# Expert gates kept in DRAM by fours of steps instead of pairs

## The chip, the cores and the metric

The kernel runs on 1 core of one Trainium2 chip. The metric is the device time of one execution in microseconds (us), as the median of several runs. Engines are named as in the profile: PE is TensorE (PEld its weight loads), DVE VectorE, ACT ScalarE, POOL GpSimd, SP the SyncE queue that issues most DMAs. L12 is line 12 of the kernel.

## What is computed

The reference is one step of a two-layer backbone over 640 tokens (128 of context, 512 latent) of width 1024. Each layer has a mixing part (gMLP and mLSTM heads) and a PEER part: every token chooses 8 x 16 of 16384 single-neuron experts by product keys. The change touches the PEER part only:

```python
idx = jnp.take_along_axis(cand_idx.reshape(T, PEER_HEADS, -1), pos, axis=-1)
gate = jax.nn.softmax(best, axis=-1).astype(h.dtype)

def block(args):
    tb, ib, gb = args
    act = jax.nn.gelu(jnp.einsum('td,thkd->thk', tb, expert_u[ib]))
    return jnp.einsum('thk,thkd->td', gb * act, expert_v[ib])
```

## The kernel before, in words

The PEER part of a layer is done in two ways at once. For 336 tokens (`NX`, the dense ones) all 16384 experts are computed, in 128 steps of 128 experts. For the other 304 (`X0` = 48 and two tiles) the rows of `peer_u` and `peer_v` are gathered one per token and choice.

**The gates.** A dense token needs a gate for each expert, zero for nearly all. They are made ahead of the 128 steps. DVE compares the chosen keys with `iota_k` (L1890, two one-hots per group of 8 tokens, in `hot1` and `hot2`), ACT and POOL multiply one of them by the gates (L1636, L2115), PE multiplies the two (L1519), and ACT evacuates the result (L1623) into `gate_s`. That is 42 groups, seven to a block of 56 tokens (`KEPT`), six blocks. Blocks 0 to 4 are stored to `gate_dram` (`store`, L1353 to L1357), and the last stays in SBUF. `gate_dram` is laid out by steps: an entry for two steps holds, for each of the 128 partitions, five blocks of 2 x 56 gates. A store thus writes 64 x 128 runs of 448 bytes, and a load of a pair (`gate_pair`, L1338) 128 rows of 2240 bytes.

**A step j.** PE makes the scores (`scores`, L1529), ACT the gelu (L1649) into `gelu_s`, DVE multiplies by the gates (`weigh`, L1901 for the 280 columns from DRAM, L1903 for the 56 kept ones) into `h_s`, and PE adds the products to PSUM (`products`, L1537 and L1542). PE's order is scores j+1, products j. The expert tiles come in through SP: `scores_of` (L1343) loads u when the scores two steps before are done (`s_a`), `values_of` (L1344) loads v when the products two steps before are done (`s_g2`). Both have two buffers. A gate pair is loaded by `gates_of`, each second step, when the weights of the pair before last are done (`s_h`). All of this stands in one queue, in the order of the code, so a wait holds everything behind it.

**The gathers.** POOL issues indirect DMAs of 128 rows of 4096 bytes, 512 KB each, into two rings of 8 slots: u (L2130) and v (L2141). DVE takes the dot of a u row (L1915) or adds a v row (L1933). Each such operation frees a slot and lets POOL issue the next row. `gathered_done` spreads the 608 operations of a layer over the steps: four a step up to step 18 (`STEADY`), then some five, fewer in the four steps of `HEAVY`. DVE does them in its program order, between `weigh(j)` and `weigh(j + 1)`.

**Into the steps.** PE's scores wait until ACT has evacuated the last group (`s_fe`). POOL's first eight u rows wait for the third store of the even buffer (`s_gst[0]`, the fifth store). SP waits for all stores, loads gate pairs 0 and 1, and then v of step 0.

Of the kernel before, what the change touches and what calls it, by code (L numbers as in the profile page):

```python
# [11 lines left out]
F32 = mybir.dt.float32  # L12
U32 = mybir.dt.uint32
# [4 lines left out]
P = 128  # L18
D = 1024
# [31 lines left out]
KEPT = NX // BLOCKS  # L51
GW = NX - KEPT
BY_BLOCK = KEPT // OCT
FIRST_AT, NEXT_AT = 0, 24
SLOTS = 80
HIDDEN = TOPK - P // SHARES
# [64 lines left out]
def build(nc, io):  # L121
# [3 lines left out]
    def sb(name, shape, dt=F32):  # L125
        return ctx.enter_context(nc.sbuf_tensor(name, shape, dt))
# [8 lines left out]
    with ctx:  # L135
# [1 line left out]
        x_res = sb("x_res", [P, TILES, D])  # L137
        y_nat = sb("y_nat", [P, TILES, D])
        big = sb("big", [P, 32000])
        gates_area = sb("gates_area", [P, 4480])  # L140
        kn_area = sb("kn_area", [P, 2560])
        ident = sb("ident", [P, P])
        ones_row = sb("ones_row", [ROWS, P])
# [18 lines left out]
        spare = sb("spare", [P, 2])  # L162
        iota_k = sb("iota_k", [P, N_KEYS])
        gate_rows = nc.dram_tensor("gate_rows", (2 * DEPTH, 2 * D), F32, kind="Internal").ap()
        gate_dram = nc.dram_tensor("expert_gates", (N_KEYS // 2, P, 2 * GW), F32, kind="Internal").ap()
        late_rows = nc.dram_tensor("late_rows", (2, P, D), F32, kind="Internal").ap()
        ctx_scores = nc.dram_tensor("context_scores", (P, 2 * D), F32, kind="Internal").ap()
        share_idx = nc.dram_tensor("share_experts", (XA, P), U32, kind="Internal").ap()
# [91 lines left out]
        eq_4 = wgate_flat  # L260

        u_ring = [big[:, 5120 + n * D:5120 + (n + 1) * D] for n in range(USLOTS - 1)] + [big[:, 19456:20480]]
        v_ring = carve(big, 21504, VSLOTS, D)
        acc = big[:, 29696:30720]
        s_cin = sem("condition_loaded")
        v_s = [big[:, 30720:31744], y_nat[:, 2, :]]
        u_s = [y_nat[:, n, :].rearrange("p (k e) -> p k e", e=P) for n in range(2)]
        gelu_s = [gates_area[:, 2560 + n * NX:2560 + (n + 1) * NX] for n in range(2)]
        h_s = [gates_area[:, 2560 + n * NX:2560 + (n + 1) * NX] for n in (2, 3)]
        g_s = [big[:, 20480:20480 + 2 * GW], gates_area[:, 2560 + 4 * NX:2560 + 4 * NX + 2 * GW]]  # L270
        part_idx = carve(kn_area, 2048, 1, P // PARTS, dt=U32)
        part_gate = carve(kn_area, 2048 + P // PARTS, 1, P // PARTS)
        a_idx = kn_area[:, 2048 + 2 * P // PARTS:2048 + 2 * P // PARTS + XA].bitcast(U32)
        a_gate = kn_area[:, 2048 + 2 * P // PARTS + XA:2048 + 2 * P // PARTS + 2 * XA]
        y_turned = carve(big, 5120, KD, 2 * P)
        fw = wgate_flat
        act_c = kn_area[:, 2432:2432 + TOPK]
# [30 lines left out]
        for l in range(DEPTH):  # L308
# [1024 lines left out]
            landed = lambda u, k, slots: l * rows_before(UNITS, 0) // slots + rows_before(u, k) // slots + 1  # L1333
            by_ranks = lambda v: v.rearrange("p (a b) -> p a b", b=TOPK)

            def gate_pair(sp, q, place):

                sp.dma_start(g_s[place], gate_dram[bass.ds(q, 1)].rearrange("a p t -> p (a t)")).then_inc(s_gs[place], 16)  # L1338

# [6 lines left out]
            with nc.Block() as block:  # L1346
                @block.sync
                def _(sp):
                    mix_sync(sp)
                    u0, v0 = stream(sp, 0, 0)  # L1350
                    u1, v1 = stream(sp, 1, 1)

                    def store(b):  # L1353

                        sp.wait_ge(s_fe, BY_BLOCK * (b + 1))
                        sp.dma_start(gate_dram[:, :, 2 * KEPT * b:2 * KEPT * (b + 1)].rearrange("q p t -> p q t"),
                                     gate_s[b % 2].rearrange("p (q s) t -> p q (s t)", s=2)).then_inc(s_gst[b % 2], 16)  # L1357

                    def scores_of(j, par, past):

                        sp.wait_ge(s_a, past)
                        stream(sp, j, par)[0]()

                    def values_of(j, par, past):

                        sp.wait_ge(s_g2, past)
                        stream(sp, j, par)[1]()

                    sp.wait_ge(s_nat, NG + 1)
                    sp.dma_start(part_rows[:, :], y_nat[0:X0, 0, :]).then_inc(s_qs, 16)  # L1370
                    for n in range(NG):
                        sp.dma_start(late_rows[n], y_nat[:, GATHERED[n], :]).then_inc(s_qs, 16)
                    sp.wait_ge(s_qs, 16 * (1 + NG))
                    for t in range(XA):
                        sp.dma_start(y_nat[SHARES * t:SHARES * (t + 1), CTX, :],
                                     part_rows[XB + t:XB + t + 1, :].broadcast_to([SHARES, D])).then_inc(s_qr, 16)
                    for part in range(PARTS):
                        sp.dma_start(y_nat[XB * part:XB * (part + 1), G0, :], part_rows[0:XB, :]).then_inc(s_qr, 16)
                    sp.wait_ge(s_s, 4 * PH)
                    sp.dma_start(gate_b.rearrange("p c d -> p (c d)"),  # L1380
                                 gate_rows[2 * l + 1:2 * l + 2].broadcast_to([P, 2 * D])).then_inc(s_grl, 16)
                    sp.wait_ge(s_sbe, 2 * PH)
                    sp.dma_start(ctx_scores.rearrange("p (g k) -> p g k", k=P), sc_b[:, 1, :, :]).then_inc(s_qs, 16)
                    sp.wait_ge(s_rk, 1)
                    u0()
                    u1()
                    v1()
                    sp.dma_start(share_idx[:, :], exp_idx[XB:X0, 0, :]).then_inc(s_qs, 16)
                    sp.dma_start(share_gate[:, :], exp_gate[XB:X0, 0, :]).then_inc(s_qs, 16)
                    for part in range(PARTS):  # L1390
                        at, slots = slice(XB * part, XB * (part + 1)), slice(P // PARTS * part, P // PARTS * (part + 1))
                        sp.dma_start(part_idx[at, 0, :], exp_idx[0:XB, 0, slots]).then_inc(s_qd, 16)
                        sp.dma_start(part_gate[at, 0, :], exp_gate[0:XB, 0, slots]).then_inc(s_qd, 16)
                    sp.wait_ge(s_qs, 16 * (NG + 4))
                    sp.dma_start(a_idx, share_idx.rearrange("t (s r) -> (t s) r", r=XA)).then_inc(s_qd, 16)
                    sp.dma_start(a_gate, share_gate.rearrange("t (s r) -> (t s) r", r=XA)).then_inc(s_qd, 16)
                    for b in range(BLOCKS - 1):
                        store(b)
                    sp.wait_ge(s_gst[0], 16 * 3)
                    sp.wait_ge(s_gst[1], 16 * 2)  # L1400
                    gate_pair(sp, 0, 0)
                    gate_pair(sp, 1, 1)
                    sp.wait_ge(s_sbe, 2 * PH + 1)
                    v0()
                    def gates_of(q, place):

                        sp.wait_ge(s_h, 2 * q - 2)
                        gate_pair(sp, q, place)

                    scores_of(2, 0, 1)  # L1410
                    with sp.Fori(0, N_KEYS // 4 - 1) as m:
                        for n in range(4):
                            scores_of(3 + 4 * m + n, 1 - n % 2, 2 + 4 * m + n)
                            if n % 2 == 0:
                                gates_of(2 + 2 * m + n // 2, n // 2)
                            values_of(2 + 4 * m + n, n % 2, 1 + 4 * m + n)
                    scores_of(N_KEYS - 1, 1, N_KEYS - 2)
                    values_of(N_KEYS - 2, 0, N_KEYS - 3)
                    values_of(N_KEYS - 1, 1, N_KEYS - 2)
                    if not final:  # L1420
                        next_weights(sp, l + 1)
                        sp.wait_ge(s_wg, (8 if first else 4) * 16)
                    else:
                        sp.dma_start(fw, io["final_norm_w"].broadcast_to([P, D])).then_inc(s_in, 16)
                        for n, t in enumerate(TAIL):
                            if t in GATHERED:
                                sp.wait_ge(s_xg, n + 1)
                            else:
                                sp.wait_ge(s_xn, n - NG + 1)
                            dst = io["y_prompt"][0] if t == CTX else io["y_sample"][0, t * P:(t + 1) * P, :]  # L1430
                            sp.dma_start(dst, y_nat[:, t, :]).then_inc(s_out, 16)
                        sp.wait_ge(s_out, 16 * TILES)
# [268 lines left out]
                def _(dve):  # L1701
# [192 lines left out]
                    def weigh(j, par, past):  # L1894

                        by_block = lambda v: v[:, 0:GW].rearrange("p (b t) -> p b t", t=KEPT)
                        dve.wait_ge(s_ge, j + 1)
                        dve.wait_ge(s_gs[j // 2 % 2], 16 * (j // 4 + 1))
                        if past is not None:
                            dve.wait_ge(s_g2, past)  # L1900
                        dve.tensor_tensor(by_block(h_s[par]), by_block(gelu_s[par]),  # L1901
                                          g_s[j // 2 % 2].rearrange("p (b s t) -> p b s t", s=2, t=KEPT)[:, :, par, :], ALU.mult)
                        dve.tensor_tensor(h_s[par][:, GW:NX], gelu_s[par][:, GW:NX], gate_s[1][:, j, :], ALU.mult).then_inc(s_h, 1)  # L1903

                    dve.wait_ge(s_sbe, 2 * PH + 1)
# [343 lines left out]
```

## Time and profile before

| | us |
|---|---|
| median of 3 runs (3691.11 to 3694.08) | 3693.1 |
| the profiled execution | 3696.82 |
| its span in the profile | 3694.7 |
| PE busy | 3577.7 |
| DVE busy | 2658.0 |
| POOL busy | 1771.5 |
| ACT busy | 547.8 |

The span goes from the first to the last instruction; the profiled execution's own time has 2.1 us around it. The 128 steps of layer 0 lie from about 693 to 1875 us, those of layer 1 from about 2496 to 3677 us. A DMA row's share is the time that packets took over 16 engines' time; packets overlap a little, so a share can be above 1.

### The profile page before, as it was taken

The numbers are of one execution on the slowest core, as the hardware profiler recorded it, in microseconds if no ns is written. First come the engines' busy times: TensorE is split into PE (matmuls) and PEld (weight loads), VectorE is DVE, ScalarE is ACT, GpSimd is POOL, SyncE is SP. The second block draws the span as 40 slices with busy tenths as digits, with TensorE's granted clock in tenths as the row PEclk, the third lists the DMA queues.
The fourth block names the chain that finished last, engine by engine and source line by source line (L and its number), as shares of the span: only waits on it lengthen the run. The fifth ranks groups of instructions, "written<-read, shape, count | busy, mean of one in ns | idle before, by whom it ended". The sixth has DMA issues, their size and how long they took to land. (4 is left out here: it accounts for less than half of the span.)

```text
span 3694.7 us, 44814 instructions
## 1 busy us (share of the span) xinstructions
PE 3577.7 (97%) x15394; PEld 2493.7 (67%) x15394; DVE 2658.0 (72%) x5798; ACT 547.8 (15%) x1123; POOL 1771.5 (48%) x1531
## 2 busy tenths in 40 slices
PE   7999999999999999999989999989999999999998
PEld 3444578777777777766655456887777777776766
DVE  4523589897888777667765356998888787777777
ACT  3212215400000000000021121170000000000001
POOL 0011006666776566666501200357567766676663
PEclk8999999999999999999999999999999999999999
DMA  9711204999999999999951013099999999999997
GB/s 396 306 65 55 103 26 123 312 405 400 408 408 408 408 408 408 409 408 408 379 208 40 29 30 124 5 237 387 400 408 408 408 408 408 408 408 408 408 409 277
DMA packets 395015, 1114.45 MB, mean 302 GB/s; under 512 B 117264, under 2 KB 123536, under 8 KB 393600
## 3 DMA queue, kind: packets, MB, share of 16 engines
q0 software_dynamic: 175104, 637.61, 43.6%
q1 hardware_dynamic: 216416, 465.72, 34.2%
q10 hardware_dynamic: 3360, 9.57, 0.7%
q8 instruction: 54, 0.88, 0.1%
q14 instruction: 81, 0.66, 0.1%
HBM read 1067.63 MB, written 45.07 MB: 301 GB/s over the span
## 5 line engine op out<-in xcount | busy, mean ns | idle before, releaser
L1529 PE MATMUL ps<-big,y_nat 128*128 128x336 f32 x4096 | 1199.1, 446 | 2.3 <-ACT big L1623 2.3
L1529 PEld LDWEIGHTS ps<-big,y_nat 128*128 128x128 f32 x4096 | 774.3, 190 | 334.6 <-ACT big L1623 2.7
L1933 DVE SCALAR_TENSOR_TENSOR big<-big,kn_area 128x1024 f32<-128x1024 f32 x608 | 782.8, 1288 | 165.9 <-DMA big<-in_peer_v,gates_area 160.1
L1915 DVE CUSTOM_DVE_ANT_0 big<-big,y_nat 128x1024 f32<-128x1024 f32 x608 | 740.3, 1224 | 127.3 <-DMA big<-in_peer_u,gates_area 124.2
L2130 POOL DMA_INDIRECT big<-in_peer_u,gates_area x512 | 656.3, 1282 | 349.0 <-DVE kn_area L1915 223.7
L2141 POOL DMA_INDIRECT big<-in_peer_v,gates_area x512 | 579.2, 1131 | 352.7 <-DVE big L1933 238.9
L1542 PEld LDWEIGHTS ps<-gates_area,y_nat 128*128 128x128 f32 x2048 | 366.9, 191 | 63.0 <-issue 62.9
L1542 PEld LDWEIGHTS ps<-gates_area,big 128*128 128x128 f32 x2048 | 363.7, 190 | 61.2 <-issue 61.2
L1649 ACT ACTIVATE gates_area<-ps 128x336 f32<-128x336 f32 x256 | 114.9, 449 | 1885.9 <-PE ps L1529 1877.3
L1542 PE MATMUL ps<-gates_area,y_nat 128*128 128x208 f32 x2048 | 383.9, 341 | 0.0
L1542 PE MATMUL ps<-gates_area,big 128*128 128x208 f32 x2048 | 381.0, 339 | 0.0
L586 PE MATMUL ps<-big 128*128 128x512 f32 x640 | 285.3, 601 | 0.0
L1537 PE MATMUL ps<-y_nat,gates_area 128*128 128x512 f32 x512 | 248.2, 608 | 31.0 <-DVE gates_area L1903 30.9
L1537 PE MATMUL ps<-big,gates_area 128*128 128x512 f32 x512 | 241.1, 593 | 0.2
L586 PEld LDWEIGHTS ps<-big 128*128 128x128 f32 x640 | 121.4, 193 | 142.1 <-issue 141.8
L1890 DVE TENSOR_TENSOR big<-iota_k,ps 128x1024 f32<-128x1024 f32 x168 | 190.6, 1223 | 5.1 <-PE ps L1519 5.1
L1519 PE MATMUL ps<-big 128*128 128x128 f32 x1344 | 167.9, 279 | 21.7 <-POOL big L2115 13.3
L2089 POOL TENSOR_TENSOR big<-big 128x48 f32<-128x48 f32 x16 | 4.3, 268 | 381.1 <-DVEq L1833 381.1
L1537 PEld LDWEIGHTS ps<-y_nat,gates_area 128*128 128x128 f32 x512 | 96.1, 192 | 126.5 <-issue 72.4
L1519 PEld LDWEIGHTS ps<-big 128*128 128x128 f32 x1344 | 155.8, 192 | 33.6 <-DVE big L1890 19.6
L1460 PE MATMUL ps<-big 128*128 128x384 f32 x512 | 170.3, 487 | 0.0
L2141 POOL DMA_INDIRECT big<-in_peer_v,kn_area x96 | 121.9, 1270 | 81.5 <-DVE big L1933 59.2
(300 smaller groups left out, 3325.5 us busy)
## 6 DMA issues: line engine op xcount, KB each, us to landing
y_nat<-in_peer_ut SPq DMA_DIRECT2D x256, 512.0 KB, 6.8
y_nat<-in_peer_v SPq DMA_DIRECT2D x128, 512.0 KB
big<-in_peer_v SPq DMA_DIRECT2D x128, 512.0 KB, 7.7
big<-in_w_mod SPq DMA_DIRECT2D x24, 2048.0 KB, 13.6
expert_gates<-big SPq DMA_DIRECT2D x10, 3584.0 KB, 16.0
big<-expert_gates SPq DMA_DIRECT2D x64, 280.0 KB, 7.5
gates_area<-expert_gates SPq DMA_DIRECT2D x64, 280.0 KB, 6.8
big<-in_w_in SPq DMA_DIRECT2D x8, 2048.0 KB, 15.8
```

The lines of the kernel that those rows point to most:

```text
L586: last = pe.matmul(ps[:, i % 2, :], h_t[:, k, t * P:(t + 1) * P], w[:, k, :], start=(k == 0), stop=(k == KD - 1))
L1460: last = pe.matmul(ps[:, g % 2, 0:ND], wq[g // PH][:, k, (g % PH) * P:(g % PH + 1) * P], h_t[:, k, 0:ND], start=(k == 0), stop=(k == KD - 1))
L1519: last = pe.matmul(pair(n % 2)[:, tt * P:(tt + 1) * P], hot2[:, n % HOTS, tt, :], hot1[:, n % HOTS, tt, :], start=True, stop=True)
L1529: last = pe.matmul(ps[:, 6 + par, 0:NX], u_s[par][:, k, :], h_t[:, k, X0:ND], start=(k == 0), stop=(k == KD - 1))
L1537: last = pe.matmul(ps[:, 4 + n, :], h_s[par][:, MOVED:NX], v_s[par][:, n * 512:(n + 1) * 512], start=first, stop=False, skip_group_check=True)
L1542: last = pe.matmul(turned(n, X0, 2 * P), v_s[par][:, n * P:(n + 1) * P], h_s[par][:, 0:MOVED], start=first and n % 2 == 0, stop=False, ski ...
L1649: act.activation(gelu_s[par], ps[:, 6 + par, 0:NX], ACT.Gelu_apprx_tanh).then_inc(s_ge, 1)
L1890: dve.tensor_tensor(hot[:, n % HOTS, :, :], iota_k[:, :].unsqueeze(1).broadcast_to(wide), ps[:, 4 + i % 2, q * P + OCT * g:q * P + OCT * ( ...
L1915: dve.tensor_tensor_reduce(out=u_ring[at], in0=u_ring[at], in1=y_nat[:, tile, :], scale=1.0, scalar=0.0, op0=ALU.mult, op1=ALU.add, accum_ ...
L1933: dve.scalar_tensor_tensor(out=acc, in0=v_ring[:, k % VSLOTS, :], scalar=wact[:, k:k + 1], in1=acc, op0=ALU.mult, op1=ALU.add).then_inc(s_ ...
L2130: pool.indirect_dma_start(out=u_ring[k % USLOTS], out_offset=None, in_=io["peer_u"][:, :], in_offset=bass.IndirectOffsetOnAxis(ap=rows_at( ...
L2141: pool.indirect_dma_start(out=v_ring[:, k % VSLOTS, :], out_offset=None, in_=io["peer_v"][:, :], in_offset=bass.IndirectOffsetOnAxis(ap=ro ...
```

## The change

`QUAD = 4`: an entry of `gate_dram` holds four steps. Stores write 32 x 128 runs of 896 bytes, loads read 128 rows of 4480 bytes, 32 a layer instead of 64. The two load buffers grow from 560 to 1120 columns. One of them, in `big`, now ends at 21600, and so the v ring, `acc` and a v buffer move up by 96 columns. The other, in `gates_area`, takes the place of a gelu buffer, which goes to `kn_area`; the part indices move behind it. Because the first buffer now reaches into `hot1` (from 21504), its first load waits for the last one-hot product (`s_f`), and v of step 0 is queued behind that. In the steps, a load is issued in the last of four steps, by a wait for weights `QUAD * q - QUAD`; the loop body has eight steps, and the last four stand behind it.

```diff
+QUAD = 4
-        gates_area = sb("gates_area", [P, 4480])
+        gates_area = sb("gates_area", [P, 4688])
-        gate_dram = nc.dram_tensor("expert_gates", (N_KEYS // 2, P, 2 * GW), F32, kind="Internal").ap()
+        gate_dram = nc.dram_tensor("expert_gates", (N_KEYS // QUAD, P, QUAD * GW), F32, kind="Internal").ap()
-        v_ring = carve(big, 21504, VSLOTS, D)
-        acc = big[:, 29696:30720]
+        v_ring = carve(big, 21600, VSLOTS, D)
+        acc = big[:, 29792:30816]
-        v_s = [big[:, 30720:31744], y_nat[:, 2, :]]
+        v_s = [big[:, 30816:31840], y_nat[:, 2, :]]
-        gelu_s = [gates_area[:, 2560 + n * NX:2560 + (n + 1) * NX] for n in range(2)]
-        h_s = [gates_area[:, 2560 + n * NX:2560 + (n + 1) * NX] for n in (2, 3)]
-        g_s = [big[:, 20480:20480 + 2 * GW], gates_area[:, 2560 + 4 * NX:2560 + 4 * NX + 2 * GW]]
-        part_idx = carve(kn_area, 2048, 1, P // PARTS, dt=U32)
+        gelu_s = [gates_area[:, 2560:2560 + NX], kn_area[:, 2048:2048 + NX]]
+        h_s = [gates_area[:, 2560 + n * NX:2560 + (n + 1) * NX] for n in (1, 2)]
+        g_s = [big[:, 20480:20480 + QUAD * GW], gates_area[:, 2560 + 3 * NX:2560 + 3 * NX + QUAD * GW]]
+        part_idx = carve(kn_area, 2464, 1, P // PARTS, dt=U32)
...
-                        sp.dma_start(gate_dram[:, :, 2 * KEPT * b:2 * KEPT * (b + 1)].rearrange("q p t -> p q t"),
-                                     gate_s[b % 2].rearrange("p (q s) t -> p q (s t)", s=2)).then_inc(s_gst[b % 2], 16)
+                        sp.dma_start(gate_dram[:, :, QUAD * KEPT * b:QUAD * KEPT * (b + 1)].rearrange("q p t -> p q t"),
+                                     gate_s[b % 2].rearrange("p (q s) t -> p q (s t)", s=QUAD)).then_inc(s_gst[b % 2], 16)
...
-                    gate_pair(sp, 0, 0)
-                    gate_pair(sp, 1, 1)
+                    gate_quad(sp, 1, 1)
                     sp.wait_ge(s_sbe, 2 * PH + 1)
+                    sp.wait_ge(s_f, GROUPS)
+                    gate_quad(sp, 0, 0)
                     v0()
                     def gates_of(q, place):
-                        sp.wait_ge(s_h, 2 * q - 2)
-                        gate_pair(sp, q, place)
-                    scores_of(2, 0, 1)
-                    with sp.Fori(0, N_KEYS // 4 - 1) as m:
+                        sp.wait_ge(s_h, QUAD * q - QUAD)
+                        gate_quad(sp, q, place)
+                    def four_steps(m, gates=None):
                         for n in range(4):
                             scores_of(3 + 4 * m + n, 1 - n % 2, 2 + 4 * m + n)
-                            if n % 2 == 0:
-                                gates_of(2 + 2 * m + n // 2, n // 2)
+                            if n == 3 and gates is not None:
+                                gates_of(m + 2, gates)
                             values_of(2 + 4 * m + n, n % 2, 1 + 4 * m + n)
+                    scores_of(2, 0, 1)
+                    with sp.Fori(0, N_KEYS // 8 - 1) as m:
+                        four_steps(2 * m, 0)
+                        four_steps(2 * m + 1, 1)
+                    four_steps(N_KEYS // 4 - 2)
...
-                        dve.wait_ge(s_gs[j // 2 % 2], 16 * (j // 4 + 1))
+                        dve.wait_ge(s_gs[j // QUAD % 2], 16 * (j // (2 * QUAD) + 1))
                         dve.tensor_tensor(by_block(h_s[par]), by_block(gelu_s[par]),
-                                          g_s[j // 2 % 2].rearrange("p (b s t) -> p b s t", s=2, t=KEPT)[:, :, par, :], ALU.mult)
+                                          g_s[j // QUAD % 2].rearrange("p (b s t) -> p b s t", s=QUAD, t=KEPT)[:, :, j % QUAD, :], ALU.mult)
```

## Rows read from the trace of the kernel before

**Rows 1.** The page, busy time of the engines and GB/s in 40 slices.
```profile
PE 3577.7 (97%) x15394; PEld 2493.7 (67%) x15394; DVE 2658.0 (72%) x5798; ACT 547.8 (15%) x1123; POOL 1771.5 (48%) x1531
...
GB/s 396 306 65 55 103 26 123 312 405 400 408 408 408 408 408 408 409 408 408 379 208 40 29 30 124 5 237 387 400 408 408 408 408 408 408 408 408 408 409 277
```

**Rows 2.** Windows: stretch, its us, engines' busy time, PE clock, DMA share, GB/s.
```profile
866.00:1817.00 951.00, 939.03 (x3727) 681.63 (x3727) 722.31 (x1267) 52.37 (x123) 619.39 (x528) 1.00 1.03 408
...
2620.00:2670.00 50.00, 50.00 (x208) 36.85 (x207) 36.76 (x69) 2.28 (x6) 29.71 (x25) 1.00 1.01 392
2670.00:3617.00 947.00, 938.49 (x3724) 682.41 (x3722) 719.76 (x1264) 52.14 (x122) 615.39 (x527) 1.00 1.03 408
3617.00:3673.00 56.00, 50.32 (x201) 36.50 (x200) 43.01 (x54) 4.29 (x9) 19.98 (x17) 1.00 0.83 303
```

**Rows 3.** Waits of PE, 700 to 1830 us and 2510 to 3690 us: total, times, longest.
```profile
PE ps L1537 <- DVE gates_area L1903: 11.8, 14, 1.6
...
PE ps L1537 <- DVE gates_area L1903: 14.3, 11, 4.4
```

**Rows 4.** Waits of DVE for gathered rows of v, 2700 to 3600 us.
```profile
DVE big L1933 <- DMA big<-in_peer_v,gates_area: 67.7, 63, 3.8
```

**Rows 5.** DMA queues and issues, 2700 to 3600 us: packets, MB, share of 16 engines.
```profile
q0 software_dynamic: 68881, 250.81, 70.0%
q1 hardware_dynamic: 34992, 116.01, 32.7%
...
gates_area<-expert_gates SPq DMA_DIRECT2D x25, 280.0 KB, 6.3
big<-expert_gates SPq DMA_DIRECT2D x24, 280.0 KB, 6.9
```

**Rows 6.** SP's queue in three stretches: 1903 to 1927, 434 to 437, 2418 to 2496.
```profile
q1 hardware_dynamic: 4777, 8.92, 102.5%
...
q1 hardware_dynamic: 151, 1.02, 81.8%
...
q1 hardware_dynamic: 41040, 18.35, 98.4%
```

**Rows 7.** Timeline of SP's queue, parts of 2647 to 3640 us: start, us, what.
```profile
2653.10 0.33 SPq L1338 DMA_DIRECT2D big<-expert_gates  x1
...
2671.20 0.33 SPq L1338 DMA_DIRECT2D gates_area<-expert_gates  x1
...
3598.75 0.33 SPq L1338 DMA_DIRECT2D gates_area<-expert_gates  x1
...
3608.13 0.33 SPq L1343 DMA_DIRECT2D y_nat<-in_peer_ut  x1
3618.57 0.33 SPq L1338 DMA_DIRECT2D big<-expert_gates  x1
3619.17 0.33 SPq L1344 DMA_DIRECT2D big<-in_peer_v  x1
...
3635.23 0.33 SPq L1338 DMA_DIRECT2D gates_area<-expert_gates  x1
```

**Rows 8.** Timeline of SP's queue, 2479 to 2500 us.
```profile
2479.86 0.37 SPq L1356 DMA_DIRECT2D expert_gates<-big  x1
2496.11 0.35 SPq L1338 DMA_DIRECT2D big<-expert_gates  x1
...
2496.98 0.43 SPq L1344 DMA_DIRECT2D big<-in_peer_v  x1
```

**Rows 9.** Timeline of the engines, 2455 to 2512 us, idle before in brackets.
```profile
2492.74 2.02 PE L1519 MATMUL ps<-big 128*128 128x128 f32 x16 [0.46 <-POOL big L2115]
...
2496.87 1.02 POOL L2130 DMA_INDIRECT big<-in_peer_u,kn_area  x1 [4.38 <-DMA expert_gates<-big]
...
2502.64 0.45 DVE L1901 TENSOR_TENSOR gates_area<-gates_area,big 128x280 f32<-128x280 f32 x1 [2.17 <-issue]
...
2505.08 1.88 PE L1537 MATMUL ps<-big,gates_area 128*128 128x512 f32 x4
```

**Rows 10.** Timeline of PE, 3380 to 3412 us.
```profile
3389.97 1.98 PE L1537 MATMUL ps<-y_nat,gates_area 128*128 128x512 f32 x4 [2.42 <-DVE gates_area L1903]
```

More of the change, by code:

```diff
@@ L262, in build @@
         u_ring = [big[:, 5120 + n * D:5120 + (n + 1) * D] for n in range(USLOTS - 1)] + [big[:, 19456:20480]]
-        v_ring = carve(big, 21504, VSLOTS, D)
-        acc = big[:, 29696:30720]
+        v_ring = carve(big, 21600, VSLOTS, D)
+        acc = big[:, 29792:30816]
         s_cin = sem("condition_loaded")
-        v_s = [big[:, 30720:31744], y_nat[:, 2, :]]
+        v_s = [big[:, 30816:31840], y_nat[:, 2, :]]
         u_s = [y_nat[:, n, :].rearrange("p (k e) -> p k e", e=P) for n in range(2)]
-        gelu_s = [gates_area[:, 2560 + n * NX:2560 + (n + 1) * NX] for n in range(2)]
-        h_s = [gates_area[:, 2560 + n * NX:2560 + (n + 1) * NX] for n in (2, 3)]
-        g_s = [big[:, 20480:20480 + 2 * GW], gates_area[:, 2560 + 4 * NX:2560 + 4 * NX + 2 * GW]]
-        part_idx = carve(kn_area, 2048, 1, P // PARTS, dt=U32)
-        part_gate = carve(kn_area, 2048 + P // PARTS, 1, P // PARTS)
-        a_idx = kn_area[:, 2048 + 2 * P // PARTS:2048 + 2 * P // PARTS + XA].bitcast(U32)
-        a_gate = kn_area[:, 2048 + 2 * P // PARTS + XA:2048 + 2 * P // PARTS + 2 * XA]
+        gelu_s = [gates_area[:, 2560:2560 + NX], kn_area[:, 2048:2048 + NX]]
+        h_s = [gates_area[:, 2560 + n * NX:2560 + (n + 1) * NX] for n in (1, 2)]
+        g_s = [big[:, 20480:20480 + QUAD * GW], gates_area[:, 2560 + 3 * NX:2560 + 3 * NX + QUAD * GW]]
+        part_idx = carve(kn_area, 2464, 1, P // PARTS, dt=U32)
+        part_gate = carve(kn_area, 2464 + P // PARTS, 1, P // PARTS)
+        a_idx = kn_area[:, 2464 + 2 * P // PARTS:2464 + 2 * P // PARTS + XA].bitcast(U32)
+        a_gate = kn_area[:, 2464 + 2 * P // PARTS + XA:2464 + 2 * P // PARTS + 2 * XA]
         y_turned = carve(big, 5120, KD, 2 * P)
@@ L1334, in build, with gate_quad @@
             by_ranks = lambda v: v.rearrange("p (a b) -> p a b", b=TOPK)
-            def gate_pair(sp, q, place):
+            def gate_quad(sp, q, place):
                 sp.dma_start(g_s[place], gate_dram[bass.ds(q, 1)].rearrange("a p t -> p (a t)")).then_inc(s_gs[place], 16)
```

## The prediction

> **What bounds the kernel now.** I read the page first. PE is busy for 97% of the span, but the line of GB/s shows two plateaus at 408, about as long as the two dense-and-gathered stages [rows 1]. Windows give their inside: from 2670 to 3617 us the DMA share is 1.03 at 408 GB/s, and in layer 0 from 866 to 1817 the same; ahead of it, in layer 1, 392 GB/s, behind it 303 [rows 2]. So each layer has a saturated stretch of about 950 us, with a little slack on either side. The other candidate is PE. Its list of waits shows no idle time in these stages but for products that wait for the weights of DVE, 11.8 us in layer 0 and 14.3 us in layer 1 [rows 3]. DVE, in its turn, waited for gathered rows of v alone for 67.7 us in 900 us [rows 4]. Transfers set the end, and PE stands right behind them: no saving of transfers in these stages can give more than 11.8 + 14.3 = 26 us.
>
> Two boundaries matter. The stretch of slack before 2670 us is where the gathers change from four operations a step to some five (STEADY = 18): there the queues have caught up, both rings are full, and what came before has no effect on what follows. The one at 3617 us is where the rows of u have run out. DMA work counts only where it is moved between these two, and less outside.
>
> **What a packet costs.** The change leaves the bytes of the gates alone and changes their cutting: loads of 128 rows of 4480 bytes instead of twice 128 of 2240, stores in runs of 896 instead of 448. The queue rows give prices [rows 5]. POOL's queue had 70.0% of 16 x 900 us = 10080 us for 250.81 MB, that is 61233 rows of 4096 bytes: 164.6 ns each, with their share of the few-byte completion writes. SP's queue had 32.7%, 4709 us. It holds 49 gate loads, 6272 packets and 14.05 MB; the other 101.96 MB are 24892 packets of 4096 bytes, 4097 us by that price. 612 us are left, 97.5 ns for a packet of 2240 (1.2 either way for the rounding). The line through the two points is 16.5 ns + 36.2 ns per 1000 bytes. It can be tested on rows that it wasn't made from [rows 6]: loads in 2048-byte runs took 102.5% of 384 us for 8.92 MB, 90.4 ns a packet (line 90.6); a store in packets of 8192 bytes 81.8% of 48 us for 1.02 MB, 314 ns (line 312.7); the gate stores in 448 bytes 98.4% of 1248 us for 18.35 MB, 30.0 ns (line 32.7). So I put a packet of 4480 bytes at 178.5 ns, against 195 for the two that it replaces. Between ends: 314/8192 x 4480 = 172 ns below, 195 above, if nothing is saved. The line is nearest, as it is right on either side.
>
> **The loads, between the two boundaries.** In layer 1 the pair loads are issued every second step: at 2653.10 before the slack ends, next at 2671.20, then on to 3598.75, 3618.57 and 3635.23 [rows 7]. The first loads are pairs 0 and 1, so the last three are 61, 62 and 63, and the one at 2671.20 is pair 11. Pairs 11 to 61, 51 of them, lie in the saturated stretch. The new load q waits for weights 4q-4 and stands after a wait for scores 4q-4: quad 5 goes at step 16, before the slack, quad 6 at step 20, quad 31 at step 120, before 3617 us. That makes 26 quads, one pair more than 51 pairs carry. Cost before: 51 x 128 x 97.5 ns = 636 us; after: 26 x 128 x 178.5 = 594 us. The difference over 16 engines is 2.65 us, and divided by the share of 1.03 (packets overlap so much) 2.6 us a layer. At 172 ns it is 3.9 us, at 195 ns a loss of 0.8 us.
>
> A rule of the Trainium skill is weighed here. The packets of 2240 follow the same line as those of 2048 and 4096 bytes, whose rows start at round addresses, so no cost of an odd start is seen [rows 5, 6]. "DMA: Bandwidth & Descriptors" (How a descriptor splits into AXI transactions) has reads start at a 256-byte boundary below an odd start, and its section Why small descriptors are slow adds some 3 cycles a packet; worked out as an estimate, 2240 bytes are 76 beats, 4480 are 145 and 4096 are 131, which puts the quad's packet at 182 ns and would make the saving about 1.8 us a layer instead of 2.6.
>
> **The tail behind 3617 us.** Pairs 62 and 63 were loaded there, 2 x 128 x 97.5/16/1.03 = 1.5 us of DMA work; after the change nothing is. But the share is 0.83, so this is worth between 0 and 1.5 us. Against it stands a wait. Before, SP waits in the first of each pair of steps for the weights of the same step, and when DVE is late, v and u are queued behind it: v follows 3618.57 at 3619.17, though PE, with the u before it gone at 3608.13, had finished that product some 4.5 us after [rows 7]. The new wait asks for weights that are a step older, which the product before v needs anyway, so it holds nobody: a v of 512 KB is asked for before 3617 instead of after, up to 1.3 us of work more in the saturated stretch. I let the two cancel and keep both for the range.
>
> **The start.** Gate 0 and v 0 are now queued behind the last one-hot product, since the wider buffer reaches into hot1 (20480 + 1120 > 21504). That product ends at 2494.8 us. In the trace of before both loads go later than that anyway: SP is held by the landing of the fifth store and issues the gates from 2496.11 on and v at 2496.98; that store went at 2479.86 [rows 8]. The store should take 4096 packets x 49 ns/16 = 12.5 us where 8192 x 30.0/16 = 15.4 were needed, so it lands near 2493. Then quad 1 goes at 2493, quad 0 at about 2495 and v 0 right behind, ahead of before; the weights want the gate at 2502.64 and the products v at 2505.08 [rows 9]. POOL's first rows, at 2496.87, come some 3 us earlier, but the first dot waits for DVE's place in its order. PE's first scores wait for ACT's evacuation, which isn't touched. Cost: 0. If the store landed as late as now, v 0 would have two times 280 KB more ahead of it: 0 to 1.4 us at 408 GB/s alone, 2.8 at half of it, all before the slack, but PE sets the pace there and would carry it on. The five other stores lie under DVE's one-hots.
>
> The 448-byte run weighs a second rule: 30.0 ns is not above the line [rows 6]. The same page (Specifications) wants at least 512 bytes, below which the DMA reads, modifies and writes; by that, 3.67 MB at 408 GB/s would land in 9 us, 6 earlier, still under other work.
>
> **What is only moved.** gelu_s, h_s, the part indices, acc and the v ring change addresses, not sizes; the multiplications of DVE read the same 280 and 56 columns; 31 instead of 62 issues of 0.33 us in SP's loop come off a queue that waits most of the time. 0 for all; bound half a microsecond.
>
> **The sum.** 2 x 2.6 = 5.2 us. The profiled execution took 3696.8 us and would take 3691.6; the runs have a median of 3693.1, so 3687.9. No change that can be told from noise is anything within 0.2%, 7.4 us: 3685.7 to 3700.5. The forecast is a small gain inside that.
>
> **Rivals.**
> 1. A long packet costs as much as its halves. Then the extra half quad costs: -5.2 becomes +1.6, 3694.7. For: no packet of this size is in the trace. Against: the 8192-byte row. 0.2.
> 2. All goes well: 172 ns, the tail's 1.5 us too, nothing lost to an earlier v: 2 x (3.9 + 1.5) = 10.8, 3682.3. For: the tail's DVE still waits for rows. Against: the line. 0.22.
> 3. The start is late: the store is no faster, v 0 costs 2.8 us a layer, and 5.2 is eaten: 3693.5. For: the store's landing is what held SP. Against: 30.0 ns against half as many packets of 49. 0.12.
> 4. Slower: bursts. A quad puts 573 KB at once into SP's queue, 1.4 us at 408 GB/s; the gathered rows behind it are late, DVE's weights too, and PE, which has no lead left in the last quarter of a layer, waits each time and doesn't win it back. PE has such waits there now, 2.42 us at 3389.97 for one [rows 10], in the steps that load a pair. Some 15 quads lie in these stretches: 15 x 1.4 = 21 us, less 5.2, 3708.9. It makes the kernel slower by 0.2% from 0.84 us a quad. Against: while the DMA engines are saturated, bytes that come early in one place are missing in another, and the total stays. 0.06.
> The forecast has 0.4.
>
> Faster by over 0.2%: rival 2, and a fifth of the forecast's own spread: 0.30. Slower: 0.05. The rest, 0.65, is within. The range goes from rival 2 to just above rival 1: 3682 to 3695.
>
> **What would show it.** Gate packets 31 x 4480 bytes instead of 62 x 2240 with SP's queue share some 0.3 points lower in the saturated stretch; stores landing in about 12.5 us, POOL's first rows before 2495; PE's waits for L1903 down by 2 to 3 us a layer and nothing new beside them. Wrong would be: a first product later than 2505.1 us, waits of PE each fourth step longer than today's, or an SP share that stays at 32.7%.

## The result and the profile after

The changed kernel takes 3646.7 us in the median of 4 runs (3644.95 to 3647.14), against 3693.1 before: ratio 0.9872, 95% interval [0.9859, 0.9884]. It is 46 us faster, where 5 were forecast. The profiled execution took 3646.26 us with a span of 3644.1, 50.6 us below the span of before.

The page of the kernel after: engines, GB/s in 40 slices, and the engines' shares of the span in the chain that ended last. It answers to [rows 1].

```profile
PE 3557.8 (98%) x15394; PEld 2492.2 (68%) x15394; DVE 2647.9 (73%) x5798; ACT 549.8 (15%) x1123; POOL 1770.1 (49%) x1531
...
GB/s 396 305 77 55 104 26 121 292 409 397 418 417 419 376 419 419 419 419 419 413 221 41 29 29 121 10 230 380 393 417 419 416 411 384 419 419 419 420 420 314
...
PE 32%; DVE 0%; issue 0%; ACT 0%; POOL 0%; ACTq 0%
```

The same line of the chain, kernel before:

```profile
PE 19%; DMA 10%; POOL 1%; issue 1%; DVE 1%; ACT 0%; DVEq 0%; ACTq 0%
```

The plateaus have risen from 408 to 419 GB/s, and the chain that ended last, which had DMA in 10% of the span before, is PE alone. That is the whole result in short: the transfers got faster, by more than the gates could give, and PE became the bound.

Where the time went is read from the places in PE's timeline where a layer's steps begin and end: the first scores (L1529, now L1538) and the first product behind the steps (L1576, now L1585). Timeline of PE, kernel before:

```profile
692.56 1.68 PE L1529 MATMUL ps<-big,y_nat 128*128 128x336 f32 x5 [1.17 <-ACT big L1623]
1879.54 2.47 PE L1576 MATMUL ps<-ident,big 128*128 128x128 f32 x16 [0.56 <-ACT big L1691]
2495.94 4.51 PE L1529 MATMUL ps<-big,y_nat 128*128 128x336 f32 x15 [1.17 <-ACT big L1623]
3681.60 2.48 PE L1576 MATMUL ps<-ident,big 128*128 128x128 f32 x16 [0.56 <-ACT big L1691]
```

Timeline of PE, kernel after:

```profile
690.23 3.94 PE L1538 MATMUL ps<-big,y_nat 128*128 128x336 f32 x13 [1.17 <-ACT big L1632]
1853.03 2.48 PE L1585 MATMUL ps<-ident,big 128*128 128x128 f32 x16 [0.56 <-ACT big L1700]
2468.20 9.31 PE L1538 MATMUL ps<-big,y_nat 128*128 128x336 f32 x32 [1.17 <-ACT big L1632]
3631.01 2.48 PE L1585 MATMUL ps<-ident,big 128*128 128x128 f32 x16 [0.56 <-ACT big L1700]
```

The steps of layer 0 went from 1187.0 to 1162.8 us, 24.2 less. Those of layer 1 went from 1185.7 to 1162.8, 22.9 less. Of the 50.6 us, 47 were won inside the 128 steps of the two layers.

Windows of the kernel after (stretch, its us, busy times, PE clock, DMA share, GB/s) answer to [rows 2]:

```profile
860.00:1800.00 940.00, 940.00 (x3745) 686.68 (x3745) 724.65 (x1280) 53.30 (x123) 622.52 (x533) 1.00 1.02 414
...
1350.00:1750.00 400.00, 400.00 (x1593) 292.22 (x1592) 297.75 (x443) 21.38 (x51) 269.92 (x225) 1.00 1.03 419
```

PE is busy for 940.00 of 940.00 us. The mean of 414 GB/s is below the plateau because the transfers now run out of work for a while (376 and 384 in the slices; before, the same slices had 408): the DMA engines have slack. The waits of DVE for rows and of SP in the 900 us from 2700 to 3600 us, kernel after (total, times, longest), answer to [rows 4]. The last line is SP's wait for the weights in the kernel before:

```profile
DVE big L1942 <- DMA big<-in_peer_v,gates_area: 11.3, 15, 2.5
DVE big L1924 <- DMA big<-in_peer_u,gates_area: 8.6, 7, 3.3
```

```profile
SPq L1344 <- PE ps L1538: 387.1, 96, 5.7
SPq L1345 <- PE ps L1551: 356.6, 97, 4.2
```

```profile
SPq L1338 <- DVE gates_area L1903: 181.8, 49, 11.0
```

DVE waits for v rows 11.3 us, where it was 67.7. And SP, which waited for the weights 49 times before, has no such row left: the new wait for weights a step older holds nobody, as forecast.

The start came out nearly as worked out. Timeline of SP's queue, kernel after, answering to [rows 8]:

```profile
2452.13 0.37 SPq L1357 DMA_DIRECT2D expert_gates<-big  x1
2465.24 0.36 SPq L1339 DMA_DIRECT2D gates_area<-expert_gates  x1
2467.11 0.35 SPq L1339 DMA_DIRECT2D big<-expert_gates  x1
2467.51 0.43 SPq L1345 DMA_DIRECT2D big<-in_peer_v  x1
```

The fifth store held SP for 13.1 us instead of 16.2 (12.5 were forecast for its packets). POOL's first row went at 2466.00, 2.2 us ahead of the first scores, where it was 0.9 behind. The products found gates and v in place.

### The profile page after: what moved, and what is told of

It reads as the page before. It is cut to its first block and busy times, and to the rows that moved or that the text cites. A ratio compares the mean times of both kernels' runs of the same rounds, so it can differ in the third digit from the quotient of the medians.

```text
span 3644.1 us, 44463 instructions
## 1 busy us (share of the span) xinstructions
PE 3557.8 (98%) x15394; PEld 2492.2 (68%) x15394; DVE 2647.9 (73%) x5798; ACT 549.8 (15%) x1123; POOL 1770.1 (49%) x1531
## 3 DMA queue, kind: packets, MB, share of 16 engines
q1 hardware_dynamic: 166240, 465.71, 32.8%
## 5 line engine op out<-in xcount | busy, mean ns | idle before, releaser
L1538 PE MATMUL ps<-big,y_nat 128*128 128x336 f32 x4096 | 1199.1, 446 | 2.3 <-ACT big L1632 2.3
L1538 PEld LDWEIGHTS ps<-big,y_nat 128*128 128x128 f32 x4096 | 774.3, 190 | 334.6 <-ACT big L1632 2.7
L1546 PE MATMUL ps<-big,gates_area 128*128 128x512 f32 x512 | 240.6, 592 | 0.0
L1546 PE MATMUL ps<-y_nat,gates_area 128*128 128x512 f32 x512 | 240.6, 592 | 0.0
L1658 ACT ACTIVATE gates_area<-ps 128x336 f32<-128x336 f32 x128 | 57.7, 451 | 1002.4 <-PE ps L1538 985.2
L1658 ACT ACTIVATE kn_area<-ps 128x336 f32<-128x336 f32 x128 | 57.8, 452 | 970.4 <-PE ps L1538 938.5
```

The source lines that it names most:

```text
L1538: last = pe.matmul(ps[:, 6 + par, 0:NX], u_s[par][:, k, :], h_t[:, k, X0:ND], start=(k == 0), stop=(k == KD - 1))
L1546: last = pe.matmul(ps[:, 4 + n, :], h_s[par][:, MOVED:NX], v_s[par][:, n * 512:(n + 1) * 512], start=first, stop=False, skip_group_check=True)
L1658: act.activation(gelu_s[par], ps[:, 6 + par, 0:NX], ACT.Gelu_apprx_tanh).then_inc(s_ge, 1)
```

## The experiments

Each ratio below is against the kernel before, run again beside the experiment (3692.8 to 3693.7 us). The packets of the steps can be priced by the queue rows as in the prediction. From 1350 to 1750 us, first the kernel before, then the one after (queue, packets, MB, share of 16 engines):

```profile
q0 software_dynamic: 30943, 112.67, 70.8%
q1 hardware_dynamic: 15262, 50.61, 32.0%
```

```profile
q0 software_dynamic: 31519, 114.78, 70.2%
q1 hardware_dynamic: 14361, 52.84, 32.3%
```

POOL's rows of 4096 bytes took 0.708 x 6400 us/27507 = 164.7 ns before and 0.702 x 6400/28022 = 160.3 after. These rows are not what the cutting of gates changed. What had changed for them is the place they are written to: with `big` counted from its start, the v ring stood at byte 86016, a multiple of 4096, and now stands 384 bytes higher. Every place in the runs below is counted from the start of `big` in this way; where `big` itself starts matters too, and comes behind the table of run 7. So there are two theories: the addresses (A), or the cut of the gate packets between them (B). All kernels below are the one before with the edit shown, unless said otherwise.

**1. The ring, acc and the v buffer moved, gates still by pairs.**

```diff
-        v_ring = carve(big, 21504, VSLOTS, D)
-        acc = big[:, 29696:30720]
-        v_s = [big[:, 30720:31744], y_nat[:, 2, :]]
+        v_ring = carve(big, 21600, VSLOTS, D)
+        acc = big[:, 29792:30816]
+        v_s = [big[:, 30816:31840], y_nat[:, 2, :]]
```

> The kernel before with one part of the change alone: the v ring, acc and the v buffer in big stand 96 columns (384 bytes) higher, gates still by pairs. The changed kernel took 3646.7 us where the one before took 3693.1, and its saturated stretch runs at 419 GB/s instead of 408, with 4096-byte packets at some 159 ns instead of 163.5. Theory A, addresses: it is the place of the ring in SBUF that makes the packets faster, so this kernel runs at 419 GB/s too and takes 3647 to 3655 us. Theory B, cutting: packets of 2240 bytes leave the DMA engines in a slower interleaving and those of 4480 don't; then this one stays at 408 GB/s and 3693 us.

Measured: 3650.8 us, ratio 0.9885 [0.9869, 0.9902], 417 GB/s from 1350 to 1750 us. Theory A: nine tenths of the gain with the gates still in pairs.

**2. The changed kernel with ring and acc moved back.**

```diff
-        v_ring = carve(big, 21600, VSLOTS, D)
-        acc = big[:, 29792:30816]
-        v_s = [big[:, 30816:31840], y_nat[:, 2, :]]
-        g_s = [big[:, 20480:20480 + QUAD * GW], ...
+        v_ring = carve(big, 21504, VSLOTS, D)
+        acc = big[:, 29696:30720]
+        v_s = [big[:, 20480:21504], y_nat[:, 2, :]]
+        g_s = [big[:, 30720:30720 + QUAD * GW], ...
```

> The changed kernel with the v ring and acc back at their old columns (gates by fours kept; the v buffer of big and the first gate buffer change places, so that everything that takes rows stands at multiples of 4096 bytes as before). Theory A, addresses: back to about 408 GB/s, and what is left is the saving that the prediction worked out, 3685 to 3690 us. Theory B, cutting: 419 GB/s and about 3647 us.

Measured: 3681.3 us, 0.9968 [0.9957, 0.9979], 410 GB/s. Theory A again, but the quads' part is larger than forecast; run 13 comes back to it.

**3 and 4. Which of the moved buffers.** In run 3 the ring and acc are at 21600 and 29792, the v buffer at 20480 and the first gate buffer at 30816. In run 4 only `v_s` has the line of run 1.

> The kernel before, gates by pairs, with the v ring and acc moved by 96 columns but the v buffer of big at a multiple of 4096 bytes (it changes places with the first gate buffer). Theory A with the ring as the cause: 419 GB/s, about 3650 us. Theory A with the v buffer as the cause, or theory B: 408 GB/s, 3693 us.

> The kernel before, gates by pairs, with nothing moved but the v buffer of big, 96 columns up. Theory A with the ring as the cause, or theory B: 408 GB/s, 3693 us. Theory A with the v buffer as the cause: 419 GB/s, about 3650 us.

Measured: run 3 3649.4 us, 0.9883 [0.9863, 0.9902], 417 GB/s: the ring is enough. Run 4 3686.3 us, 0.9981 [0.9971, 0.9991], 410 GB/s: the v buffer, which takes 7% of the bytes, gives a small part. More bytes at such a place give more, but not in proportion: 7% of them gave 1.5 GB/s, the ring's third 8.6.

**5. acc alone**, at 29792, with v buffer and gate buffer as in run 3 and the ring at 21504.

> The kernel before, gates by pairs, with acc alone 96 columns higher; the v ring stays at column 21504, a multiple of 4096 bytes. The run with ring and acc moved took 3649.4 us at 417 GB/s. Theory A1: the writes of the DMA engines into the ring are what its place changes, acc is of no account: 3693 us, 408 GB/s, less a little if any. Rival A2: it is DVE's addition, which reads ring and acc at like addresses, that gets in the way of the writes; then acc's place parts the two as well and this one takes some 3650 us at 417 GB/s.

Measured: 3688.5 us, 0.9986 [0.9975, 0.9997], 409 GB/s. A2 falls: it is not that DVE's addition reads ring and acc at like addresses. DVE's additions take 1288 to 1290 ns each in the kernel before and in runs 3 and 6 alike. The table of run 7 comes back to the small gain.

**6. Both rings moved alike**, so that u and v rows meet at like addresses again.

```diff
+        gate_s = [carve(big, 5120 + n * (N_KEYS * KEPT + 96), N_KEYS, KEPT) for n in range(2)]
+        u_ring = [big[:, 5216 + n * D:5216 + (n + 1) * D] for n in range(USLOTS - 1)] + [big[:, 19552:20576]]
+        v_ring = carve(big, 21600, VSLOTS, D)
...
+        g_s = [big[:, 20576:20576 + 2 * GW], ...
```

> The kernel before, gates by pairs, with both rings, acc and the v buffer of big 96 columns higher, so that u rows and v rows land at like addresses again, only not at multiples of 4096 bytes. Theory R, relative: what costs is that rows of u and of v are written at the same low address bits at once; the expected rate is then back near 408 to 412 GB/s and 3680 to 3693 us. Rival S, start: what costs is a row that starts at a multiple of 4096 bytes; then this one is at least as fast as with the v ring alone moved, 417 to 421 GB/s and 3645 to 3650 us.

Measured: 3648.8 us, 0.9879 [0.985, 0.9908]. Theory R falls: the distance between the rings is nothing. S holds in that the start of each ring counts; which starts are slow, S has too narrow, as runs 7 to 16 show. Window and POOL's queue of this run, 1350 to 1750 us:

```profile
1350.00:1750.00 400.00, 400.00 (x1596) 292.80 (x1595) 297.58 (x443) 21.31 (x51) 270.05 (x224) 1.00 1.03 419
```

```profile
q0 software_dynamic: 31628, 115.16, 70.4%
```

It has the changed kernel's rate, 419 GB/s, with gates by pairs.

**7 to 11 and 16. By how much the ring is moved**, everything else as in run 3: `v_ring` starts at 21504 plus 16, 512, 32, 64, 128 and 48 columns, acc right behind it.

> As the run with ring and acc alone moved (3649.4 us, 417 GB/s), but by 16 columns, 64 bytes, in place of 384. If any difference of address parts the writes, 417 GB/s and 3650 us; if two packets must be apart by more than a burst of some hundred bytes, between 408 and 415 GB/s and 3655 to 3693 us.

> As the run with ring and acc alone moved, but by 512 columns, 2048 bytes. If the conflict is among low address bits below 2048, which this step leaves alike, it is as slow as before: 408 GB/s, 3693 us. If rows conflict because they start at the same place of a 4096-byte grid, 417 GB/s or more and 3650 us.

> Ring and acc of the kernel before moved by 128 bytes (64 gave 409 GB/s, 384 gave 417, 2048 gave 408). Theory S512: what counts is where a row starts within 512 bytes, slow at 0 and near it; 128 is then between, 410 to 417 GB/s, 3650 to 3688 us. Theory S256: what counts is the start within 256 bytes, where 384 is 128; then this is as good as 384: 417 GB/s, 3650 us.

> The same by 256 bytes. Theory S512: the middle of 512, 417 GB/s or more, 3650 us or less. Theory S256: again a round start, 408 GB/s and 3693 us.

> The same by 512 bytes. Theories S512 and S256: a round start, 408 GB/s and 3693 us. Rival: only a start at a multiple of 2048 is slow, and 64 was too near to it; then 417 GB/s and 3650 us.

> Ring and acc of the kernel before moved by 192 bytes. 64 and 256 bytes gave 409.2 GB/s, as acc's move without the ring did, so nothing; 128 and 384 gave 417. If every start that isn't near a round one is good, 417 GB/s and 3650 us; if only 128 past a multiple of 256 is, 409 GB/s and 3688 us.

| run | ring moved by, bytes | place of the ring in the partition, within 256 | first gate buffer, the same | GB/s, 1350 to 1750 us | PE's waits for L1903, us | median, us | ratio |
|---|---|---|---|---|---|---|---|
| before | 0 | 128 | 128 | 408 | 30.9 | 3693.1 | |
| 7 | 64 | 192 | 0 | 409 | 26.9 | 3689.5 | 0.9988 [0.9977, 0.9999] |
| 9 | 128 | 0 | 0 | 417 | 4.1 | 3656.5 | 0.9898 [0.9869, 0.9927] |
| 16 | 192 | 64 | 0 | 409 | 27.8 | 3688.4 | 0.9986 [0.9976, 0.9996] |
| 10 | 256 | 128 | 0 | 409 | 28.7 | 3688.3 | 0.9989 [0.9978, 1.0] |
| 3 | 384 | 0 | 0 | 417 | 0.7 | 3649.4 | 0.9883 [0.9863, 0.9902] |
| 11 | 512 | 128 | 128 | 408 | 30.4 | 3692.4 | 0.9997 [0.9986, 1.0009] |
| 8 | 2048 | 128 | 128 | 408 | 32.5 | 3693.7 | 1.0004 [0.9992, 1.0015] |

The pattern is plain: 128 and 384 bytes are fast, 0, 64, 192, 256, 512 and 2048 are not. Counted from the start of `big`, a fast start is 128 bytes past a multiple of 256, and nothing near it will do.

**But `big` does not start at a multiple of 256 itself.** The allocator of the program gives a partition's first free bytes, from 16384 on, to four constants of the framework, 32 bytes apart. The trace shows them being set:

```profile
0.26 0.10 POOL L2241 MEMSET const-float32-0.0<- 128x1 f32 x1 [0.26 <-issue]
0.29 0.10 POOL L2241 MEMSET const-float32-1.0<- 128x1 f32 x1
0.32 0.10 POOL L2241 MEMSET const-bfloat16-1.0<- 128x1 bf16 x1
0.34 0.10 POOL L2241 MEMSET const-uint8-127<- 128x1 uint8 x1
```

Behind them come `x_res` at byte 16512, `y_nat` at 36992 and `big` at 57472. Nothing ahead of `big` differs between the kernels here, and 57472 is 224 x 256 + 128. So the third column reads the other way round: in the partition, the fast starts (runs 3 and 9) are the multiples of 256 bytes, and every start 64, 128 or 192 bytes past one is slow. The "round" places of the expectations were round only within `big`. In the kernel before, no buffer for rows stood at a multiple of 256: both rings, the tiles of u and v in `y_nat` and `big` and both gate buffers were 128 bytes past one. The allocation is read from the program; the traces hold no addresses, and no run moved `big` as a whole.

The fourth column goes with the last GB/s: where the ring is at a slow place, the kernels with the first gate buffer at a multiple of 256 have 409 and those without have 408. Run 13 below has 409 with its first gate buffer at 128 and the second one moved, so this is a likely reading and no more. Windows of run 8 and of run 9, 1350 to 1750 us:

```profile
1350.00:1750.00 400.00, 391.85 (x1548) 282.58 (x1547) 287.15 (x419) 20.35 (x50) 254.82 (x213) 1.00 1.03 408
```

```profile
1350.00:1750.00 400.00, 400.00 (x1595) 292.52 (x1594) 297.16 (x439) 21.35 (x51) 270.74 (x224) 1.00 1.03 417
```

The DMA share is 1.03 in both. Only the packets got shorter: a share cannot show such a thing, GB/s at full share does. And the shortening isn't confined to the packets that land in the moved ring. By the packet records of the traces (completion writes left out), SP's packets of 4096 bytes, all of which still go to unmoved places in run 3, took 163.4 ns before and 160.1 there; POOL's took 163.5 and 159.9. So moving one ring made the packets to other places shorter too.

Run 9 has the rate of run 3 and 7 us more in the median. The profiled executions are 6.1 us apart, 4.3 of them inside the steps, where PE waits twice for 4.1 us in all, and 1.8 outside. Why wasn't looked into.

**12. The u ring alone**, by 384 bytes (the lines of run 6 for `gate_s`, `u_ring` and `g_s`; the v ring stays).

> The kernel before with the u ring moved by 384 bytes and the v ring left at its round start (the second gate block moves with it, since the ring lies over it). If any ring with an odd start relieves the DMA engines in proportion to the rows it takes, this one is like the v ring moved alone: 417 GB/s, 3650 us. If there is something about the v ring or DVE's additions from it, 408 to 410 GB/s and 3685 to 3693 us.

Measured: 3651.5 us, 0.9885 [0.9856, 0.9913], 417 GB/s. Another buffer that takes as many rows serves as well, so it is nothing about the v ring. The second ring adds little to the first: 417 GB/s with either, 419 with both (run 6).

**13. What the quads are worth by themselves**: run 2 with pairs.

```diff
-        v_s = [big[:, 30720:31744], y_nat[:, 2, :]]
-        gelu_s = [gates_area[:, 2560 + n * NX:2560 + (n + 1) * NX] for n in range(2)]
+        v_s = [big[:, 20480:21504], y_nat[:, 2, :]]
+        gelu_s = [gates_area[:, 2560:2560 + NX], kn_area[:, 2048:2048 + NX]]
+        h_s = [gates_area[:, 2560 + n * NX:2560 + (n + 1) * NX] for n in (1, 2)]
+        g_s = [big[:, 30720:30720 + 2 * GW], gates_area[:, 2560 + 3 * NX:2560 + 3 * NX + 2 * GW]]
+        part_idx = carve(kn_area, 2464, 1, P // PARTS, dt=U32)
...
```

> The kernel with quads and an unmoved ring (3681.3 us, 410.0 GB/s) with one thing undone: the gates go by pairs again. Everything that is moved there stays: gate buffers, gelu, h, v buffer at round places or where they are. If the prediction's term for the cutting is right, the difference between the two is 2 x 2.6 = 5 us: 3686.5 us here, 408.4 to 409.5 GB/s. If the quads are worth what that run gained over the kernel before, 12 us, this one takes 3693 us.

Measured: 3689.0 us, 0.999 [0.9981, 1.0], where the same with quads took 3681.3: the cutting gives 7.8 us and the places of the other buffers 4 (the medians of the kernel before beside the two differ by 0.5 us). PE's waits for the weights are 28.1 us here and 24.6 with quads. The forecast's term was 5.2.

**14. Quads, and every buffer in `big` that takes rows at 128 within 256 of `big`**, so at a multiple of 256 in the partition: `u_ring` and `gate_s` as in run 6, `v_ring` at 21728, acc at 29920, `v_s` at 30944, `g_s` at 20576.

> The changed kernel with the u ring moved too, so that rings, v buffer of big and first gate buffer all start 128 bytes into a block of 256. DMA would run at 419 GB/s or a little above with all packets of 4096 bytes at 159 ns. The steps of the changed kernel have no wait of PE left, so theory: PE sets the time and nothing is gained, 3645 to 3648 us. Rival: transfers still set it somewhere, then 3640 us or less.

Measured: 3647.6 us, 0.9876 [0.9859, 0.9892], 420 GB/s; DVE's wait for v rows falls further. The time does not: PE sets it. The tiles in `y_nat` and the gate buffer in `gates_area` are still off a multiple of 256, so 420 is not shown to be the ceiling.

**15. The place of reading.** The tiles of u and v are streamed from DRAM tensors that begin 32 elements late; all places in SBUF are those of before.

```diff
+    io["peer_ut"] = io["peer_ut"][32:32 + DEPTH * N_EXPERTS * D].rearrange("(e p d) -> e p d", p=P, d=D)
+    io["peer_vs"] = io["peer_vs"][32:32 + DEPTH * N_EXPERTS * D].rearrange("(n d) -> n d", d=D)
```

> The kernel before with all places in SBUF as they were, but the DRAM tensors that the tiles of u and v are streamed from start 128 bytes late, 27% of the bytes. Theory D: only where a row is written counts; 408.4 GB/s and 3693 us. Theory L: what counts is that source and destination start alike; then the tiles gain as the v buffer did (7% of the bytes gave 1.5 GB/s): 412 to 415 GB/s and 3655 to 3675 us.

Measured: 3694.5 us, 1.0004 [0.9993, 1.0014], 408 GB/s. Window of run 15, 1350 to 1750 us:

```profile
1350.00:1750.00 400.00, 391.20 (x1544) 281.88 (x1543) 287.30 (x419) 20.35 (x50) 254.33 (x213) 1.00 1.03 408
```

Where these tiles are read from is nothing to the rate. Their destinations in `y_nat` and `big` are 128 bytes past a multiple of 256, and now the reads start 128 bytes late too, so theory L, that like starts on both sides help, falls as far as the DRAM tensors begin at a multiple of 256, which no run shows. What an off start of the source costs when the destination is at a multiple of 256 wasn't tried, nor was anything for the gathered rows.

A page of the Trainium skill bears on this. "DMA: Bandwidth & Descriptors" (How a descriptor splits into AXI transactions) says that an AXI transaction that reads must start at a multiple of 256 bytes, so a descriptor that starts elsewhere pays beats (of 32 bytes) for bytes that it doesn't use. It states this for reads only. On the writing side the runs agree with it in direction: runs 3, 6, 9 and 12, with a ring at a multiple of 256 in the partition, are the fast ones. As an estimate by the page's count, carried over to writes, a row of 4096 bytes that starts 128 past a multiple takes 132 beats instead of 128, 3.1% more; 164.7 ns against 160.3 is 2.7% more. The count doesn't fit in detail: it would make a start 64 past cheaper than one 128 past and a start 192 past dearer, and runs 16, 10 and 7 all have 409 GB/s. For reads, run 15 shows no cost, beside writes that were off as well.

## Why the prediction was wrong

**The step that failed** is the one under "What is only moved": acc, the v ring and the other buffers "change addresses, not sizes", 0 for all, bound half a microsecond. I looked at what the engines read and write there and not at the transfers that land there. The ring takes a third of the bytes of the saturated stretch (half of POOL's 250.81 MB of 367 [rows 5]), and 96 columns took it from 128 bytes past a multiple of 256 to a multiple of 256 in the partition. With acc and the v buffer moved too that is worth 42 us (run 1, 3693.1 to 3650.8); ring and acc with the first gate buffer give 44 (run 3). No row of before could price it, since every buffer for rows stood at an off place there; the prediction should have said so, and kept a range for it, as it did for the packet size.

**The rule was in the prediction, on one side only.** It weighed the cost of an odd start and saw none, because packets of 2240 bytes lie on a line with those of 2048 and 4096 bytes "whose rows start at round addresses" [rows 5, 6]. Its count of beats went by the starts in DRAM. On the SBUF side the loads compared all landed 128 bytes past a multiple of 256, so the line had the same off start in each of its loads and could not show what it costs.

**The cap was too low as well.** "No saving of transfers can give more than 26 us" came from PE's idle time [rows 3]. One window ended at 1830 us, short of the last product of layer 0, which waited too: over both layers the wait is 30.9 us. And some wait seems to hide inside busy time: the products from `y_nat` took 608 ns a matmul and now 592, so 248.2 became 240.6 us with no change in work. The steps gained 24.2 + 22.9 = 47 us. The right cap was the count of steps by PE's own pace: one step without a wait is 9.05 us, as between these rows of the kernel after, so 128 take 1158 of the 1162.8 us measured.

```profile
3598.60 4.68 PE L1538 MATMUL ps<-big,y_nat 128*128 128x336 f32 x16
...
3607.65 4.68 PE L1538 MATMUL ps<-big,y_nat 128*128 128x336 f32 x16
```

**The loads, between the boundaries**: right in its mechanism, a little small: 5.2 us forecast, 7.8 measured (runs 13 and 2). The price of the long packet: by the same way as in the prediction, 0.323 x 6400 us, less 11360 packets of 4096 at 160.3 ns, leaves 246 us for 11 loads, 175 ns each; 178.5 were forecast, the lower end was 172. Where the rest lies, in the tail, in the earlier v or elsewhere, isn't told apart. The sign that I named for it did not show: SP's share from 2700 to 3600 us is 32.7% with quads (run 2) and 32.8% with pairs (run 13), not 0.3 points apart. SP moved more bytes in that time, 117.17 MB against 116.60, which covers part of it.

**The start** held: the store landed earlier, quad 1, quad 0 and v 0 went earlier, no first product waited. So did the wait in SP's loop. Rivals 3 and 4, the late start and the bursts, did not come: PE has no wait for the weights left (L1912, which was L1903), and in run 2, where transfers still are the bound, its longest is 3.7 us against 4.8 before.

**Rival 2** named the right direction and lacked the cause of the 46 us. Its 3682.3 is near what the kernel takes with quads and the ring left alone (3681.3), but 4 of those 12 us come from the places of the other buffers (run 13), so that is in part luck.

**What stays open** is the mechanism behind a start at a multiple of 256. It isn't the reading side of the tiles, nor like addresses of ring and acc, nor two rings that collide. A row of 4096 bytes takes some 4 ns longer when rings start elsewhere, the same 64, 128 and 192 bytes past, and packets to other places take longer too. All of this was measured with the DMA engines saturated. A kernel whose tiles as a whole are moved by 128 bytes, `y_nat` with them, would be the plain test of the reading by partition addresses; it was not run.

## What to carry to other kernels

A buffer that takes DMA rows has a place as well as a size. Where DMA bandwidth is the bound, let each large destination start at a multiple of 256 bytes in the partition, and count from the start of the partition: a place that is round within its tile need not be, since here the tile itself began 128 bytes past a multiple. It cost 96 columns here and gave 1.15% (run 1). When a diff moves a buffer "only", ask who writes it, and put a price range on the move if the trace has no row at the new place. And take the bound behind the bound from the pace of an undisturbed step, not from a sum of idle times.

## What the runs showed of the hardware

- Rows of 4096 bytes written to SBUF at full load, with their completion writes: 164.7 ns with all starts 128 bytes past a multiple of 256 in the partition, 160.3 with both rings at multiples of 256 (runs before and 6; 0.704 x 6400/28115). The rate goes from 408 to 419 GB/s, 420 with the quads and the other row buffers of `big` at such places too (run 14).
- One of two equal rings at a multiple of 256 gives most of it, 417 GB/s (runs 3 and 12); 7% of the bytes give 410 (run 4). With one ring moved, packets that land elsewhere get shorter as well, 163.4 to 160.1 ns (run 3).
- Starts 64, 128 and 192 bytes past a multiple of 256 are alike, 409 GB/s with the first gate buffer at a multiple (runs 16, 10 and 7).
- The start of the streamed rows in DRAM, 27% of the bytes, made no difference at 128 bytes, with all destinations off a multiple of 256 (run 15).
- Packets of 8192, 4096, 2240 and 2048 bytes lie on one line, some 16 ns and 36 ns per 1000 bytes; packets of 448 bytes took 30.0 ns, 2.7 under it, and those of 4480 bytes 175 in the kernel after [rows 5, 6].
